# Laying out all big weights of a two-block decoder kernel as the ring reads them: one run of 16 KB per partition for a slab, one of 8 KB for a piece of w_ada

## The reference

```python
u = rms_norm(h, norm_g[l])
proj = jnp.einsum('bsd,de->bse', u, w_in[l])
...
h = h + jnp.einsum('bse,ed->bsd', mix, w_out[l])
...
mod = jax.nn.silu(c.astype(F32)) @ w_ada + b_ada
p = h @ w_in
gates = jax.nn.sigmoid((h @ w_gate + b_gate).astype(F32))
merged = merged + gates[..., i * d:(i + 1) * d] * (y @ w_branch[i])
x = x + (gate1[:, None, :] * (merged.astype(x.dtype) @ w_o)).astype(x.dtype)
...
return (jax.nn.silu(xb @ w_exp_gate[e]) * (xb @ w_exp_up[e])) @ w_exp_down[e]
```

## Time and profile before

| | |
|---|---|
| time, median of 3 runs | 2047.63 us (2043.04 to 2049.13) |
| time of the profiled execution | 2049.79 us |
| its span | 2048.0 us |
| busy share: PE, DVE, ACT, POOL | 81%, 26%, 16%, 2% |
| mean granted clock of TensorE | 0.907 of full speed |
| DMA packets, bytes | 94726, 582.38 MB |
| of these, queue 1 (SP) / queue 0 (POOL) | 530.16 MB / 50.33 MB |

### The profile page before, as it was taken

The page is one execution under the profiler, slowest core; times in us unless marked ns, Lnnn a source line. Parts: engine busy times, 40 slices in busy tenths (PEclk is TensorE's granted clock), DMA queues, the critical chain, the costliest instruction groups (busy, mean ns, idle before and its releaser), DMA issues.

```text
span 2048.0 us, 26820 instructions
## 1 busy us (share of the span) xinstructions
PE 1649.8 (81%) x12123; PEld 1153.7 (56%) x12123; DVE 528.2 (26%) x975; ACT 320.4 (16%) x637; POOL 50.2 (2%) x79
## 2 busy tenths in 40 slices
PE   7998989999999986556656599999999656555566
PEld 6875877887888842222222188878888222221222
DVE  5776872633011130000000035231023100000001
ACT  2332312312210010000000042212111000000001
POOL 0011100100000000000000001000000000000000
PEclk9998999999999987778788799999999888777888
DMA  7798754303346669999999942134484899999995
GB/s 254 254 352 336 289 194 155 124 3 124 124 165 242 251 274 429 432 429 430 433 430 429 419 141 84 44 124 144 144 336 157 379 429 433 431 433 430 431 430 236
DMA packets 94726, 582.38 MB, mean 284 GB/s; under 512 B 12024, under 2 KB 14864, under 8 KB 81680
## 3 DMA queue, kind: packets, MB, share of 16 engines
q1 hardware_dynamic: 79312, 530.16, 63.5%
q0 software_dynamic: 13056, 50.33, 6.5%
q10 hardware_dynamic: 2240, 0.11, 0.1%
HBM read 579.54 MB, written 1.05 MB: 283 GB/s over the span
## 4 chain that ended last, share of the span: by engine, by line
PE 51%; DMA 26%; issue 5%; DVE 1%; ACT 1%; SPq 0%
DMA expert_slots<-in_w_exp_down 19%; PE ps L1308 13%; PE ps L2466 11%; PE ps L2105 8%; PE ps L2118 4%; DMA expert_slots<-in_w_exp_up 3%; DMA expert_slots<-in_w_exp_gate 3%; PE ps L2143 3%; PE ps L2481 2%; PE ps L1311 1%; PE ps L1773 1%; PE ps L1785 1%; PE ps L1791 1%; PE ps L1743 1%; PE ps L1535 1%
## 5 line engine op out<-in xcount | busy, mean ns | idle before, releaser
L2466 PE MATMUL ps<-expert_slots,gathered 128*32 128x512 f32 x2048 | 281.3, 712 | 298.3 <-DMA expert_slots<-in_w_exp_up 143.5
L2466 PEld LDWEIGHTS ps<-expert_slots,gathered 128*32 128x32 f32 x2048 | 73.7, 128 | 497.1 <-issue 340.7
L1308 PE MATMUL ps<-h,ring 128*128 128x256 f32 x1216 | 275.5, 382 | 0.0
L1308 PEld LDWEIGHTS ps<-h,ring 128*128 128x128 f32 x1216 | 227.5, 190 | 37.0 <-issue 4.5
L2582 DVE TENSOR_TENSOR gate_up_rows<-silu_rows,ps 128x512 f32<-128x512 f32 x16 | 11.0, 687 | 777.3 <-issue 652.7
L2466 PE MATMUL ps<-expert_slots,gate_up_turned 128*32 128x512 f32 x1024 | 139.3, 693 | 56.1 <-DMA expert_slots<-in_w_exp_down 48.2
L2105 PE MATMUL ps<-h,ring 128*128 128x256 f32 x768 | 166.7, 379 | 0.0
L2105 PEld LDWEIGHTS ps<-h,ring 128*128 128x128 f32 x768 | 145.9, 190 | 19.8
L262 PE MATMUL ps<-u,ring 128*128 128x256 f32 x640 | 145.3, 382 | 0.0
L262 PEld LDWEIGHTS ps<-u,ring 128*128 128x128 f32 x640 | 119.9, 190 | 20.4 <-issue 3.0
L2466 PEld LDWEIGHTS ps<-expert_slots,gate_up_turned 128*32 128x32 f32 x1024 | 34.5, 124 | 149.6 <-issue 80.2
(11 more groups left out here) (466 smaller groups left out, 1655.8 us busy)
## 6 DMA issues: line engine op xcount, KB each, us to landing
expert_slots<-in_w_exp_up SPq DMA_DIRECT2D x32, 4096.0 KB, 28.8
expert_slots<-in_w_exp_down SPq DMA_DIRECT2D x32, 4096.0 KB, 21.6
expert_slots<-in_w_exp_gate SPq DMA_DIRECT2D x28, 4096.0 KB, 27.4
ring<-in_w_in SPq DMA_DIRECT2D x31, 2048.0 KB, 8.9
ada_ring<-in_w_ada POOLq DMA_DIRECT2D x48, 1024.0 KB, 7.9
ring<-in_w_gate SPq DMA_DIRECT2D x12, 2048.0 KB, 7.8
expert_slots<-in_w_exp_gate SPq DMA_DIRECT2D x8, 2048.0 KB, 7.5
ring<-in_w_branch SPq DMA_DIRECT2D x6, 2048.0 KB, 7.6
```

The costliest lines, as they stand in the source:

```text
L1308: ins = nc.tensor.matmul(k.ps[:, IN_BANK[t], 0:S], slab[:, j, c:c + w], k.h[:, j, :], start=j == 0, stop=j == ND - 1)
L2466: ins = nc.tensor.matmul(k.ps[r, bank, :], left[:, j, r], slab[:, i, j, :], start=j == 0, stop=j == slab.shape[2] - 1)
```

## The change

The arrays are rearranged before the launch so that what one DMA reads lies together for each partition. `first_slabs` and `mix_slabs` now build arrays instead of views: for every slab, each partition has its 4096 floats in one run (16 KB; the first slab of a layer 8 KB). A piece of `w_ada` is one run of 8 KB per partition where it was two of 4 KB. The runs were 2 KB for `w_in`, `w_in_2`, `w_gate_2` and `w_o_2` (1 KB in the first slab of a layer), and 4 KB for `w_out` and `w_branch_2`. The bytes, the destinations, the waits and the order of the issues stay. `w_dtf` still comes from `w_in` as it was.

```diff
+def by_partition(rows):
+    return rows.reshape(-1, P, rows.shape[1]).transpose(1, 0, 2).reshape(P, -1)
...
-def first_slabs(k):
-    w_in = k.io["w_in"][0].rearrange("(k p) c -> p k c", p=P)
-    w_out = k.io["w_out"][0].rearrange("(m p) c -> p m c", p=P)
+def first_slabs(w_in, w_out):
...
-    return [w_in[:, :, a:a + 512] for a in at] + [w_out[:, 4 * r:4 * r + 4, :] for r in OUT_ROWS]
+    return np.stack([by_partition(w_in[:, a:a + 512]) for a in at]
+                    + [by_partition(w_out[4 * P * r:4 * P * (r + 1)]) for r in OUT_ROWS])
...
-            n, c = slabs[s].shape[1:]
-            sp.dma_start(k.ring[:, s % SLOTS, :].rearrange("p (k c) -> p k c", k=n), slabs[s]).then_inc(sem.ring_loaded[s % SLOTS], 16)
+            sp.dma_start(k.ring[:, s % SLOTS, :], slabs[s]).then_inc(sem.ring_loaded[s % SLOTS], 16)
...
-        ada = io["w_ada_2"].rearrange("l (p j r) (g c) -> l g j p r c", r=ADA_ROWS, j=ND // ADA_ROWS, c=ADA_COLS)
+        ada = io["w_ada_2"].rearrange("l g j p (r c) -> l g j p r c", r=ADA_ROWS)
...
+def mix_slab(k, l, i):
+    a = max(0, i * SLAB - SLAB // 2)
+    return k.io["mix_slabs"][l, :, a:(i + 1) * SLAB - SLAB // 2]
...
-            kk, c = slabs[i].shape[1:]
-            dst = k.ring[:, n % SLOTS, 0:kk * c].rearrange("p (k c) -> p k c", k=kk)
-            sp.dma_start(dst, slabs[i]).then_inc(k.mix_loaded[n % SLOTS], 16)
+            src = mix_slab(k, l, i)
+            sp.dma_start(k.ring[:, n % SLOTS, 0:src.shape[1]], src).then_inc(k.mix_loaded[n % SLOTS], 16)
...
+    arrays["first_slabs"] = first_slabs(arrays["w_in"][0], arrays.pop("w_out")[0])
+    mixers = [arrays.pop(name) for name in ("w_in_2", "w_gate_2", "w_branch_2", "w_o_2")]
+    arrays["mix_slabs"] = np.stack([mix_slabs(*(a[l] for a in mixers)) for l in range(LAYERS)])
+    a = arrays["w_ada_2"].reshape(LAYERS, P, ND // ADA_ROWS, ADA_ROWS, N_ADA // LAYERS, ADA_COLS)
+    arrays["w_ada_2"] = np.ascontiguousarray(a.transpose(0, 4, 2, 1, 3, 5)).reshape(
+        LAYERS, N_ADA // LAYERS, ND // ADA_ROWS, P, ADA_ROWS * ADA_COLS)
```

More of the change, by code:

```diff
@@ L358, in first_loads @@
     nc, io, sem = k.nc, k.io, f.sem
-    slabs = first_slabs(k)
+    slabs = io["first_slabs"]
     @block.sync
@@ L1213, with mix_slabs @@
 BRANCHES = (1, 2, 0)
-def in_slabs(k, l):
-    w = k.io["w_in_2"].rearrange("l (k p) c -> l p k c", p=P)
+def mix_slabs(w_in, w_gate, w_branch, w_o):
     r0, c0 = 4 * MW, 4 * MW + N_K * P
@@ L1222, in in_slabs @@
     spans += [(i * MW, MW) for i in range(4)] + [(c0 + i * MW, MW) for i in range(3)]
[L1223 to L1231, removed]
-    for n in BRANCHES:
-        slabs += [w_gate[l, :, :, n * D + i * 512:n * D + (i + 1) * 512] for i in range(2)]
-        slabs += [w_branch[l, n]]
-    return slabs + [w_o[l, :, :, i * 512:(i + 1) * 512] for i in range(2)]
+    slabs = [by_partition(w_in[:, a:a + n]) for a, n in spans]
+    for n in BRANCHES:
+        slabs += [by_partition(w_gate[:, n * D + i * 512:n * D + (i + 1) * 512]) for i in range(2)]
+        slabs += [by_partition(w_branch[n])]
+    return np.concatenate(slabs + [by_partition(w_o[:, i * 512:(i + 1) * 512]) for i in range(2)], axis=1)
+def mix_slab(k, l, i):
+    a = max(0, i * SLAB - SLAB // 2)
+    return k.io["mix_slabs"][l, :, a:(i + 1) * SLAB - SLAB // 2]
 IN_TILES = [(0, 0, P, None), (0, P, P, None)]
@@ L1370, in layer_loads @@
     l, sem, past, io = y.l, y.sem, y.past, k.io
-    slabs = mix_slabs_2(k, l)
     @block.sync
```

## The result

The kernel after takes 2062.53 us (median of 7 runs, 2060.54 to 2067.13) beside 2048.02 us before in the same session (7 runs): ratio 1.0070, 95% interval 1.0058 to 1.0081. The change costs 14.5 us. The profiled execution took 2060.74 us, 10.95 more than that of before; its span is 2058.9 us.

A forecast was written before the change was run, and what follows sets the result against it. It took untouched `w_exp` transfers to bound two long stretches and PE the rest. Terms 10.4 + 2.6 = +13.0 us on the profiled 2049.79 gave 2062.8, median 2060.6 us; 8 in 10 range 2045 to 2068.

The forecast's parts named there:

- (a): Slabs into `ring`: each lands 0.3 to 0.5 us sooner, but behind PE work, so 0.
- (b): Start: `w_dtf` runs alternate one for one with 16 KB runs, so PE's first tile starts at 27.0 us, +10.4 us.
- (c): First tile: PE's clock is at the lower level after the long idle time, +2.6 us (between 0 and 5).
- (d): First block's `w_ada` pieces in 8 KB runs beside slabs: gain and loss balance, 0, between -11 and +10 us.
- (e): SP no longer blocks 5.44 us at L377; constants come earlier but DVE needs them only after the first tile: 0.
- groups of small runs per turn: Rival at the start: ten or more `w_dtf` runs pass per turn, the 1.4 us wait goes, 2046.2 us; chance 0.06.
- long runs cut short: Rival at the start: engines switch inside a 16 KB run, nothing at the start moves, 2047 us; chance 0.13.
- Pieces sooner: Rival, first block: DVE's `w_ada` waits shrink, -11 us: 2036.6 without the start loss (0.08), 2049.6 with it (0.10).
- pieces later: Rival, first block: a slab ahead of an awaited `w_ada` piece costs +5 us or more, 2066 to 2071; chance 0.11.

The follow-up runs named there:

- experiment 10: Kernel before with only the layers' slabs in runs of 16 KB: 2047.86 us, ratio 0.9998.
- experiment 1: Kernel after with `w_dtf` laid out as one run of 1280 bytes per partition, a single DMA: 2051.33 us, ratio 1.0015.
- experiment 5: Kernel after with slab 2 and what follows held back until `w_dtf` has landed: 2058.69 us, ratio 1.0053.
- experiment 4: Kernel after with the first block's slabs in runs of 4 KB: 2047.88 us, ratio 0.9997.
- experiment 6: Kernel after with 32 products of no use on PE ahead of its wait for `w_dtf`: 2064.69 us, ratio 1.0089.
- experiment 7: Kernel after with 24 products of no use on PE ahead of its wait for `w_dtf`: 2062.35 us, ratio 1.0066.
- experiment 2: Kernel before with only `w_dtf` laid out as one run of 1280 bytes per partition: 2047.13 us, ratio 0.9994.
- experiment 8: Kernel before with only the pieces of `w_ada` in runs of 8 KB: 2041.78 us, ratio 0.9958.
- experiment 9: Kernel before with only the first block's slabs in runs of 16 KB: 2074.8 us, ratio 1.0127.
- kernel 11: Kernel before with `w_dtf` in one run per partition, `w_ada` pieces in 8 KB and layers' slabs in 16 KB runs: 2039.96 us, ratio 0.9967.

## Why the prediction was right

2060.6 us was forecast and 2062.53 measured; the profiled execution was to take 2062.8 and took 2060.74. The mechanism of the start is the one forecast. That the totals came so close is partly luck: in the profile the start cost 14.6 us instead of 13.0, 1.2 more were lost before 118 us and 1.1 regained around `q`, none of them forecast, and 3.7 came back at L284.

(a) Slabs 0: shown by experiment 10 for the layers' 44. For all of them, the tile `ring` has no wait on a transfer in the kernel after, and its idle time of "issue" is again 30.2 us.

(b) The turn, +10.4: right in its mechanism, a little small. The first tile was put at 27.0 us and came at 28.47, +11.8. The second issue landed 26.2 us after it was made, not 24; queue 10 had 62 packets from 9 to 11 us where some 50 were named. Experiments 1 and 5 show that the delay comes from what is queued beside the many small runs of `w_dtf`. Experiment 4 shows what the sum left out: the engines don't finish together, and one with a few runs left holds PE.

(c) The clock, +2.6: the tile took 6.3 us instead of 3.65, +2.7, and experiments 6 and 7 show that idleness caused it. Too strong was the statement of (b) that no slack absorbs the delay. In the profiled executions a gain at the start of 2.6 us (experiment 7) is gone after the wait for `q` and one of 5.4 (experiment 5) is down to 2.3, while one of 16.2 us (experiment 1) arrives whole, 17.6 us. One profile of each can't settle how much of a start is absorbed there.

(d) The pieces, 0 between bounds of -11 and +10: 14.0 us of waits, against the 14.3 forecast. The zero is a balance. The longer pieces alone gave a ratio of 0.9958 (6.8 us), the longer slabs alone cost about 12 us beyond the start; both move the share that I had worked out. They don't add up (26.2 us for the slabs less 6.8 for the pieces is 19.4, and the change costs 14.5): beside slabs of 16 KB the longer pieces have a third of the bytes where the old ones had a fifth. The balance is not quite even: with the start mended in both, the median of experiment 1 lies 4.2 us above that of experiment 2. It also varies: 3.7 us came back at L284 in the profiled execution, where experiment 10 has 3.2 without any change there, while the medians (+14.5 us for a start of +14.6) show nothing given back. Which slab meets which piece probably differs from one execution to the next; that is argued, not shown.

(e) SP stops blocking: `first_constants` is issued in 0.53 us instead of 5.44, slab 2 at 10.6 us instead of 16.4, and no engine was seen to gain by it. As (b) had it, the early slab 2 only adds to what `w_dtf` alternates with: experiment 5.

The rivals: groups of small runs per turn, and long runs cut short, both fell at 61 packets to 62 from 9 to 11 us, with 0.82 MB in the 61. The first is what the rule of the Trainium skill ("DMA: Bandwidth & Descriptors", "Queues, rings and completion order") would give if it were applied descriptor for descriptor here; the runs show single descriptors alternating at 2, 4, 8 and 16 KB. Pieces sooner and pieces later were both real mechanisms, each on its own: experiments 8 and 9. In the change they nearly cancel.

## What to carry to other kernels

Before lengthening the runs of a big load, look at what shares the DMA engines with it at each place: in every pair of queues measured here each got a run for a run, so the load with the shorter runs loses bytes in that proportion. A small load of many tiny runs that an engine waits for has to become few runs first, or be through first. Lengthen the runs of the load that is waited for (`w_dtf`, `w_ada`) and leave the one that is ahead of its use as it is: kernel 11, which leaves the first block's slabs alone, is 7.0 us faster than the kernel before of its session.

## What the runs showed of the hardware

- While both queues hold work, the alternation is strict: from 9 to 11 us 342 to 341 packets with 2 KB runs, 191 to 191 with 4 KB, 104 to 104 with 8 KB, 61 to 62 with 16 KB.
- With no long run beside them (experiment 5, from 20 us), runs of 32 and 64 bytes pass at 842 packets in 2 us; beside 16 KB runs, at 62.
- The end of a load of many runs is set by single engines: with 4 KB runs all but 16 packets of `w_dtf` were through by 18 us, and the last of them held PE to 22.4.
- One kernel's executions can lie 13 us apart (2043.1 to 2056.07 in experiment 1), which one profile does not show; with the same first block, PE was 3.2 us apart at 293 us (experiment 10 and the kernel before).
